# Projections of a hybrid decoder step in seven block products instead of eight, with K and V apart and the branch inputs through DRAM

## The reference

```python
h = rmsnorm(x, g_mix_pre)
q, k, v, cb, cc, cu, ga, gb = split(h @ w_in)      # 1024,128,128, 3 x 1024, 2 x 2048 columns
q, k = rope(q), rope(k)
a = window_attention(q, k, v, sinks)               # blocks of 128, 16 heads, 2 KV heads
b_out = cb * causal_dwconv(cc * cu)                # 3 taps
merged = sigmoid(ga + b0) * (a @ w_attn_branch) + sigmoid(gb + b1) * (b_out @ w_conv_branch)
x = x + rmsnorm(merged @ w_o, g_mix_post)
up, gt = split(rmsnorm(x) @ w_ffn_up)              # 2 x 5632 columns
x = x + rmsnorm((gelu(causal_dwconv(up) + b) * gt) @ w_ffn_down)
x = x + sigmoid(x @ w_ple_gate) * (p @ w_ple)
```

## Time and profile before

| what | us |
|---|---|
| median of 3 runs (2893.45 to 2894.02) | 2893.95 |
| the profiled execution | 2893.35 |
| its span, first to last instruction | 2891.7 |
| PE busy | 2784.8 (96%) |
| VectorE busy | 2024.4 (70%) |
| ScalarE busy | 1231.9 (43%) |
| GpSimd busy | 64.8 (2%) |
| mean granted clock of TensorE | 0.983 of 2.4 GHz |

### The profile page before, as it was taken

One profiled execution on the slowest core, in us unless ns is written; L12 is line 12 of the kernel. 1 busy time (PEld: TensorE's weight loads), 2 busy tenths in 40 slices (PEclk: granted clock), 3 DMA queues, 4 the chain that ended last, 5 costly groups with the idle time before them and its releaser, 6 DMA issues. The chain is left out here.

```text
span 2891.7 us, 57855 instructions
## 1 busy us (share of the span) xinstructions
PE 2784.8 (96%) x22023; PEld 2719.5 (94%) x22023; DVE 2024.4 (70%) x3439; ACT 1231.9 (43%) x2172; POOL 64.8 (2%) x67
## 2 busy tenths in 40 slices
PE   6999999999999999989999999999999999999789
PEld 6989999999999999978999999999998999989589
DVE  6355454333333358888888888888889788899988
ACT  4223323222222234545555555555555453445344
POOL 4110000000000000000000000000000000000000
PEclk8999999999999999999999999999999999999799
DMA  4222222233333333352333233332334243334343
GB/s 172 84 75 76 75 78 80 88 91 91 91 91 91 91 105 109 130 201 95 119 110 131 99 131 111 118 130 99 131 104 176 97 147 107 106 117 142 141 174 131
DMA packets 129393, 327.67 MB, mean 113 GB/s; under 512 B 15001, under 2 KB 35105, under 8 KB 126288
## 3 DMA queue, kind: packets, MB, share of 16 engines
q1 hardware_dynamic: 128992, 325.68, 33.3%
q0 software_dynamic: 288, 0.67, 0.1%
HBM read 297.13 MB, written 30.41 MB: 113 GB/s over the span
## 5 line engine op out<-in xcount | busy, mean ns | idle before, releaser
L907 PE MATMUL pair<-o_hi,v_hi 128*128 128x260 f32 x4270 | 1216.2, 285 | 36.0 <-DVE y_sb L1865 10.9
L907 PE MATMUL pair<-o_hi,v_lo 128*128 128x260 f32 x4270 | 1210.8, 284 | 0.0
L907 PE MATMUL pair<-lo,v_hi 128*128 128x260 f32 x3050 | 866.0, 284 | 0.0
L1132 ACT ACTIVATE v_hi<-s_raw 128x512 fp32r<-128x512 f32 (+1 forms) x944 | 585.8, 622 | 636.9 <-PE pair L907 612.2
L907 PEld LDWEIGHTS pair<-o_hi,v_hi 128*128 128x128 f32 x4270 | 808.7, 189 | 41.7 <-issue 23.2
L907 PEld LDWEIGHTS pair<-o_hi,v_lo 128*128 128x128 f32 x4270 | 809.8, 190 | 0.0
L1693 DVE TENSOR_TENSOR v_lo<-s_raw,v_hi 128x512 fp32r<-128x512 f32 (+1 forms) x944 | 638.2, 677 | 174.7 <-ACT v_hi L1132 139.5
L1402 DVE TENSOR_TENSOR w_lo<-w_raw,w_hi 128x512 fp32r<-128x512 f32 x328 | 238.9, 732 | 556.4 <-ACT w_hi L987 556.4
L907 PEld LDWEIGHTS pair<-lo,v_hi 128*128 128x128 f32 x3050 | 578.2, 190 | 0.2
L987 ACT ACTIVATE w_hi<-w_raw 128x512 fp32r<-128x512 f32 x328 | 206.7, 631 | 664.0 <-PE pair L660 646.7
L660 PE MATMUL pair<-h_hi,w_hi 128*128 128x260 f32 x2112 | 435.1, 287 | 22.0 <-DVE h_lo L1424 14.0
(11 more groups left out here) (219 smaller groups left out, 2722.7 us busy)
## 6 DMA issues: line engine op xcount, KB each, us to landing
s_raw<-in_sstream SPq DMA_DIRECT2D x308, 512.0 KB, 4.9
w_raw<-in_wstream SPq DMA_DIRECT2D x328, 256.0 KB, 2.6
s_raw<-in_sstream SPq DMA_DIRECT2D x32, 384.0 KB, 3.1
f_scr<-fo SPq DMA_DIRECT2D x88, 130.0 KB, 1.9
x_scr<-y_sb SPq DMA_DIRECT2D x8, 1040.0 KB, 4.2
raw<-f_scr SPq DMA_DIRECT2D x7, 1040.0 KB, 5.6
raw<-in_x SPq DMA_DIRECT2D x4, 1040.0 KB, 6.5
ple_scr<-ple_sb SPq DMA_DIRECT2D x4, 1040.0 KB, 4.8
```

Source lines behind the costliest of these rows:

```text
L907: mm = pe.matmul(out, wt[:, slot, kk * P:kk * P + P], r[:, k, :], start=j in (0, 1, 3) and k == 0 and n == 0, stop=k == nk - 1 and n == 2, ...
L1132: nc.scalar.activation(v_hi[:, n % 4, 0:width], src, ACT.Copy).then_inc(v_hi_rdy, 1)
```

## The change

The projections of Q, conv and gates become a set of 32 units of seven block products (set 0 with `U_O` = 32 units: 2 of gates, 4 of Q, 12 of conv, 14 of gates), written out in a line instead of in loops. K and V are made first, in native fp32, from rows of x as they arrive, x times the gain but not yet times the norm; the norm is then multiplied into the 16 rows in place (`h_row`), and the set begins. Everything that the attention and the branches need, and that stayed in SBUF before, goes through DRAM scratch: rotated Q (`q_scr`), b (`b_scr`), sigmoided gates (`g_scr`), attention output (`a_scr`). The attention is cut into 16 quarter blocks (two head pairs each) in place of 8 half blocks, one in each of the units of `ATT`. The two branches are 32 steps of 48 matmuls in the old three-matmul form, first all of the conv branch, then all of the attention branch. The squares of x are summed by VectorE and no longer by GpSimd, the rotation (cosine part) too; GpSimd issues the DMAs of the attention.

```diff
+U_Q, U_CONV, U_SIG = 2, 6, 18
+U_O, N_O = 32, KD // 2
+def kind(u):
+    return "g" if u < U_Q or u >= U_SIG else "q" if u < U_CONV else "CuB"[(u - U_CONV) % 3]
+ATT = {U_CONV + 7: 0, U_CONV + 10: 1, **{U_SIG + n: n + 2 for n in range(14)}}
...
 @block.tensor
+            for k in range(KD):
+                pe.wait_ge(x_rdy, k + 1)
+                for n, w in enumerate(quarter_of(k)[:2]):
...
+                        mm = pe.matmul(pair[2 + n][:, h, 0:HALF], w[:, quarter_of(k)[2]], x_half(k, h),
+                                       start=k == 0, stop=k == KD - 1, skip_group_check=True)
+                mm.then_inc(kv_used, 1)
...
+            def between(u):
+                if u - 1 in range(U_Q, U_CONV):
+                    r = 2 * (u - 1 - U_Q)
+                    return {0: lambda: rotate(r), 2: lambda: rotate(r + 1)}
+                if u == U_CONV + 1:
+                    return {0: v_turn, 1: lambda: rotate(KA)}
+                if u == U_CONV + 3:
+                    return {0: sample_scores, 5: sample_turn}
+                if u == U_CONV + 4:
+                    return {1: sample_values}
+                if u in ATT:
+                    n = ATT[u]
+                    return {-1: lambda: scores(n), 3: lambda: turn(n), 5: lambda: values(n)}
+                return {}
...
-            units(0)
+            first_unit(0)
+            for u in range(1, U_O):
+                unit(0, u, u % 2, between(u))
...
 @block.scalar
+            def exponentials(n):
+                act.wait_ge(m_ready, n + 1)
+                for h in range(4):
+                    nc.scalar.activation(s_sb[:, h, :], s_sb[:, h, :], ACT.Exp,
+                                         bias=small[:, 1, h:h + 1],
+                                         accum_out=small[:, 3, h:h + 1])
+                nc.scalar.activation(small[:, 4, 0:4], small[:, 2, 0:4], ACT.Exp)\
+                  .then_inc(e_ready, 1)
...
+            def h_evac(u, i):
+                d, k = d_h[u % 2], kind(u)
+                if u and kind(u - 1) == "g" and i in (0, 1):
+                    sigmoid_g(u - 1, i)
+                if i == (0 if is_first(u) else 1):
...
+                    copied(u, 0, d[:, 0, 0:HALF], r1_out)
+                if i == 3:
+                    copied(u, 1, d[:, 1, HALF:T], r5_out)
+                if i == 5:
+                    copied(u, 2, d[:, 0, HALF:T], r2_out)
+                if k == "B" and i == 2:
+                    conv_first((u - U_CONV) // 3)
...
+                if u in ATT and i == 4:
+                    exponentials(ATT[u])
+                if u in ATT and i == 9:
+                    turned(ATT[u])
+            by(0, h_evac)
...
 @block.vector
+            def h_row(k):
+                dve.wait_ge(kv_used, k + 1)
+                dve.tensor_tensor(x_tile(k), x_tile(k), two(rstd[:, :]), ALU.mult).then_inc(h_rdy, 1)
...
+            def h_evac(u, i):
+                if U_Q < u <= U_CONV:
+                    r = 2 * (u - 1 - U_Q)
+                    if i == 2:
+                        sine(r)
+                        cosine(r)
+                    if i == 3:
+                        turn_q(r)
+                    if i == 6:
+                        sine(r + 1)
+                        cosine(r + 1)
+                        turn_q(r + 1)
...
+                if k == "B":
+                    m = (u - U_CONV) // 3
+                    if i in (0, 1):
+                        conv_z(m, i)
+                    if i in (3, 6):
+                        conv_taps(m, i // 6)
+                if u and kind(u - 1) == "B" and i in (0, 1):
+                    conv_b((u - 1 - U_CONV) // 3, i)
...
+                if u in ATT:
+                    if i in (0, 1):
+                        masked(ATT[u], i)
+                    if i == 2:
+                        shifts(ATT[u])
+                    if i == 6:
+                        probabilities(ATT[u])
+                    if i == 12:
+                        attention_out(ATT[u])
+                sums(u, i, d[:, 0, 0:HALF], d[:, 0, HALF:T], d[:, 1, HALF:T])
...
 @block.sync
+            for u in range(U_O - 1):
+                h_store(u - 1)
+                load(r_of(u) + 2)
...
+            br_load(0)
...
+            br_load(1)
+            for m in range(NBR):
+                if m + 2 < NBR:
+                    sp.wait_ge(br_free, m + 1)
+                    g_load(m + 2)
+                if m % 4 == 3:
+                    load(R_BR + m // 4 + 2)
```

More of the change, by code:

```diff
@@ L109, in build @@
         r_raw4 = region(4 * HB)
[L110 to L131, removed]
+        r_op = region(10 * HB)
+        r_w = region((8 + 1) * KH * P * 4 + 2 * 4 * 4 * P * 4)
+        r_g = region(KD * XB)
+        r_c = top[0]
+        o = [r_w]
         def sub(name, shape, dt=f32):
@@ new lines, in _ @@
+            u = U_O - 1
+            h_store(u - 1)
+            for i in range(2):
+                sp.wait_ge(h_stored[i], 16 * stores_before(u - 1 + (i != (u - 1) % 2)))
+            sp.wait_ge(v_used, h_of(u, 1, 1) + 1)
+            br_load(0)
+            sp.wait_ge(b_rdy, KA)
+            g_load(0)
+            g_load(1)
+            load(r_of(u) + 2)
+            h_store(u)
+            sp.wait_ge(v_used, h_of(u, 6, 1) + 1)
+            for i in range(2):
+                sp.wait_ge(a_stored[i], 16 * 8)
+                sp.wait_ge(h_stored[i], 16 * stores_before(U_O + i))
@@ L565, in _ @@
             x_store(3)
-            load(u + 3)
+            load(r_of(U_UP) + 1)
             ple_store(2)
@@ L653, in _ @@
         def _(pe):
-            def products(acc, slot, kk, rhi, rlo, k, start, stop):
-                w = slice(kk * P, kk * P + P)
-                for wt, r, first, last in ((w_hi, rhi, True, False), (w_hi, rlo, False, False),
-                                           (w_lo, rhi, False, True)):
-                    for h in range(2):
-                        mm = pe.matmul(pair[acc][:, h, 0:HALF], wt[:, slot, w],
-                                       r[:, k, h * HALF:(h + 1) * HALF],
-                                       start=start and first, stop=stop and last)
-                return mm
@@ new lines, in _, with rotate @@
+            pe.wait_ge(sq_added, KD - 1)
+            pe.wait_ge(pool_set, 3)
+            for h in range(2):
+                mm = pe.matmul(pair[1][:, h, 0:HALF], ones[:, :],
+                               sqacc1[:, h * HALF:(h + 1) * HALF], start=True, stop=True)
+            mm.then_inc(sum_ready, 1)
+            def rotate(r):
+                u = U_Q + r // 2
+                if r < KA:
+                    for n in ((c11_out, c12_out), (c22_out, c21_out))[r % 2]:
+                        pe.wait_ge(n, u + 1)
+                    src = d_h[u % 2][:, r % 2, :]
+                else:
+                    src = k_in
+                pe.wait_ge(kv_out, 2)
+                if r:
@@ L1250, in _ @@
+            v_high(BR_S + 3)
+            sigmoid_g(U_O - 1, 0)
+            sigmoid_g(U_O - 1, 1)
+            warm(ACT.Sqrt, 2)
+            for m in range(NBR):
+                if m + 2 < NBR:
+                    v_high(BR_S + 2 * m + 4)
+                    v_high(BR_S + 2 * m + 5)
+                if 4 <= m < 4 + KA:
+                    br_high(1, m - 4)
+            by(1, wo_evac)
             y_square(U_UP - 1, 2)
@@ new lines, in masked @@
+            def masked(n, g):
+                if g == 0:
+                    dve.wait_ge(mask_ready[n >= 4], 16)
+                    if n:
+                        dve.wait_ge(pT_ready, 2 * n)
+                dve.wait_ge(sc_ready, 2 * n + g + 1)
+                for v in range(2):
+                    h = 2 * g + v
+                    ins = dve.tensor_tensor_reduce(
+                        s_sb[:, h, :], bank[g][:, v * 256:(v + 1) * 256], mask_blk[:, :],
+                        SCALE, -3.0e38, ALU.add, ALU.max, small[:, 0, h:h + 1])
@@ L1833, in unit @@
                 n = s_of(u, 0)
-                more = not last or u == U_UP - 1
+                ahead = 16 if u == U_O - 1 else 14 if last and u != U_UP - 1 else 18
                 for i in range(14):
-                    if i < 10 or more:
+                    if i + 4 < ahead:
                         v_low(n + i + 4)
@@ L2222 @@
                             range(16 * c + nk, 16 * c + 2 * nk)))
-    sparts.append(quads(tiles(wg, 0), tiles(wg, 1), lower, upper))
+    sparts.append(pairs_of(v["w_ple_gate"][0]))
     sstream = np.concatenate(sparts)
```

1401 lines of the change are left out of this document (660 added, 741 removed).

## The result

| what | before | after |
|---|---|---|
| median of 5 runs on the same chip | 2893.45 (2891.96 to 2894.02) | 2908.03 (2903.39 to 2908.42) |
| profiled execution, span | 2891.7 | 2905.9 |
| mean granted clock of TensorE | 0.983 | 0.970 |

The account below looks back on a forecast made before the run. TensorE (PE) was taken to set the pace nearly everywhere. w_o would start at 968.5 + 63 + 26 + 18 = 1075.5 us, 14 later than 1061.7, giving 2893.95 + 14 = 2908 us; eight-in-ten range 2840 to 2926.

Parts of the forecast that it names:

- Waits for the probabilities: Attention quarters: TensorE stands 13 times 4.2 us with a table load in the chain, 3 times 2.8 without: 63 us.
- Half clock: Attention units: after each of the 13 long waits matmuls run slow, 2 us each: 26 us, bounds 0 and 33.
- Convolution, rotations, samples: First stage: added VectorE steps make small waits, mainly for the sum before half 12: 18 us, bounds 0 and 30.
- the four in the B units: Four units with two convolution taps and small steps on VectorE: about 2.4 us late each, 9 us.
- Start and matmuls: First stage without new waits: first row at 44.4 us, third unit at 111.5, w_o at 968.5, 93 us less.
- 605 + 67 + 184 + 1: From the third unit to w_o: 30 units of 20.16 us, kept TensorE work, the branches, and 1 at w_o.
- the clock stays: Rival, chance 0.25: attention waits come but the clock does not fall, and small waits cost 5 us less: 2877 us.
- The test set for it: Sign for the clock rival: whether the granted clock is over 0.95 in 650 to 1000 us.
- the steps fit: Rival, chance 0.12: ScalarE and VectorE get ahead, TensorE stands under 1 us in an attention quarter: 2827 us.
- A late start: Rival, chance 0.07 shared with starved units: K and V at half clock throughout, ending 24 us later: 2932 us.
- starved units: Rival sharing chance 0.07 with a late start; the DMA estimate said that without cover a unit waits for its 5 us load.
- a load costs double: Rival, chance 0.06: ScalarE drains another 1.28 us for each of 13 table loads, 17 us: 2925 us.

Follow-up runs that it names:

- experiment 7: Changed kernel with probabilities at step 4 of VectorE's list, transposes after product 4, and gates by tanh instead of sigmoid: 2813.81 us.
- experiment 3: Changed kernel with the probabilities at step 4 instead of 6 of VectorE's list, before two weight slots' low parts: 2839.26 us.
- experiment 1: Changed kernel with the first set's gates taking Exp in place of Sigmoid (another function, only timed), so no table switches: 2871.31 us.
- experiment 5: Changed kernel with ScalarE starting the exponentials at step 3 of its list instead of step 4: 2906.98 us.
- experiment 6: Changed kernel with VectorE's taps, second rotations and sample copies moved behind the sum of the lower right block: 2897.9 us.
- experiment 8: Changed kernel with probabilities at step 4, transposes after product 4, tanh gates, and VectorE's other steps behind the lower right sum: 2805.6 us.
- experiment 4: Changed kernel with both moves: transposes after product 4 and probabilities at step 4 of VectorE's list: 2828.45 us.

## Why the prediction was right

The periods put the terms apart. In units with gates:

| run | wait for probabilities | period | over 23.55 | over the wait |
|---|---|---|---|---|
| 7 (no wait, no loads) | 0 | 23.55 | 0 | 0 |
| 3 | 1.55 | 25.40 | 1.85 | 0.3 |
| 1 | 2.45 | 27.44 | 3.89 | 1.4 |
| the change | 3.88 | 29.59 | 6.04 | 2.2 |

(a period is the distance between the first and the thirteenth quarter of these units, by 12).

*Waits for the probabilities.* Predicted 13 of 4.2 us with a table load in the chain and 3 of 2.8: 63. Measured 13 of 3.88 and 3 of 2.45: 57.7. The count was 0.3 us too high for each of them: from the start of the high part (662.43) TensorE stands after 4.3 us and not after 4.1, so the 0.2 taken off for the semaphore was most of it, and it starts again after 8.2 and not 8.3. The difference between the kinds is 1.43 us, against my 1.4. The chain was the right one: load, exponentials, two high parts, two low parts, probabilities. Experiment 1 takes out the first link, 3 the low parts, and 5 shows that moving only the exponentials inside the chain brings nothing.

*Half clock.* Predicted 2 us for each long wait, 26 in all, and none for the three shorter ones. By the last column it is 2.2 for each of the 13, 28 us, of which up to 0.3 is the restart that experiment 3 shows at full clock. The three of 2.45 us had it as well, some 1.4 each by experiment 1, 4 us. The term is 32 instead of 26, and the step that failed a little is the reading of the earlier trace rows: I let the first attention block, with 2.82 us and no fall, speak for the three. Such a wait was not always followed by it (11 of 16 times in experiment 1), so that these 4 us could have been less in another run. So both attention terms together are 90 us, and 89 were forecast.

*Convolution, rotations, samples.* Predicted 18 us. The listed waits in these units are 11.0 + 2.1 + 0.2 = 13.3 us, and 13 restarts of about 0.3 (an estimate, from experiment 3) make 17. One stretch of half clock, which I did not forecast, lies behind waits of 2.08 and 0.96 us at the samples' softmax (0.59 granted from 289 to 291 us, 0.56 from 291 to 293), about 1.5 more: 19. Their parts were less good: the four in the B units were 1.6 us, not 2.4, the rotations 0.6, not 0.9. Experiment 6 shows that they come from the steps ahead of the sum.

*Start and matmuls.* The first row of h was used at 45.3 us (44.4 predicted), half 12 of the second unit began at 105.0 (44.4 + 60.9 + 1.3 = 106.6 by the prediction's terms) and the third unit, 24 matmuls on, at 109.5 (111.5), the branches took 184.5 us from 890.9 to 1075.4 (184), and w_o began at 1075.4 (1075.5). From there it is 1830.5 us to the end, as before. In experiment 8, the third unit starts at 109.3 us and w_o at 972.7. Of these 863.4 us, 4.1 are listed waits and about 1.5 half clock behind the softmax, which leaves 858; the prediction's 605 + 67 + 184 + 1 is 857. A unit without attention takes 20.4 us there (three units with one quarter are 425.52 - 361.15 = 64.37 us, less 23.55, by two), with a wait of 0.24 us in every third; 20.2 was said. So matmuls and kept work were right, and the start was 2 us shorter than forecast.

*The rivals.* That the clock stays would have given 2877. The test set for it, over 0.95 from 650 to 1000 us, was a poor one: some 110 us of that stretch are branches at 1.00, and its mean is 0.95. In the attention units alone (640 to 900 us) it is 0.92, and it fell behind all thirteen long waits. That the steps fit would have given 2827; experiment 4 makes that case, with 0.66 us of waiting in a quarter: 2828. A late start is out, since K and V ran from 8.0 to 38.7 us, and so are starved units: no wait of TensorE from 100 to 1060 us was ended by a DMA. That a load costs double is out: the load at 663.08 begins 0.02 us after the high part's end, it lasts 1.28, and its removal shortens the wait by 1.43. The drain of 1.38 us that the Trainium skill (ScalarE: Activation LUTs, What ACT_TABLE_LOAD costs) adds to each switch is not seen here. The rule of the Trainium skill (the same page, Table sets), to batch by set, holds: the loads cost 37 us of the changed kernel by experiment 1, with the clock that follows. There are 27 of them from 500 to 900 us, 13 before exponentials and 14 before sigmoids; the prediction's "26 between 600 and 900" had the stretch wrong.

So the change does bring what its count of matmuls says, 93 us up to w_o, and 2 more at the start. The new order gives back 109: some 58 in waits for the probabilities, 32 in half clock and restarts behind them and 19 in the small waits. That w_o began within 0.1 us of the forecast is luck: the start was 2 us too long and the waits together 2 us too short. Most of what was given back was order and one function's table, not work: experiment 7, with both moves and tanh, keeps every matmul and gets some 93 us back.

## What to carry to other kernels

Work that is moved from a queue with free time into a densely pipelined unit is priced by the chain through all engines' lists, from the link that makes it possible to the one that wants it; here 2.3 us of a 3.9 us wait were unrelated steps that had slack of their own. Before splitting such a chain, look at where the consumer asks: one line that let TensorE ask a product later was worth 76 us. And count what follows a long stand of TensorE as part of its price: 3.88 us cost 6.0.

## What was not expected

Waits of 2.45 us were followed by the 1.2 GHz level in all three places of the change, in two of three in experiment 6 and in 11 of 16 in experiment 1, where two waits of one length, 26 us apart, went both ways. In experiment 5 one of two waits of 2.48 us was followed by it, and one of 3.03 us, which ended at 490.38, was not. Before, a stand of 2.82 us had not been either; there by stretches of 2 us (us, TensorE's busy time and records, granted clock, DMA share, GB/s):

```profile
212.00:214.00 2.00, 2.00 (x10) 1.00 0.29 111
214.00:216.00 2.00, 2.00 (x15) 1.00 0.00 0
```

None of the thirteen waits of 1.55 us in experiment 3 was, and every one of the 3.88 us of the change and of the 3.94 us of experiment 5. So from about 2.4 to 3 us the length of the wait alone doesn't decide it, and no run here settles what else does.

A wait of 0.66 us in the view was worth 1.16 us a unit (experiments 4 and 7), so the view understates short waits. And the steps of experiment 6 gave 10.1 us on the change and 8.2 on top of experiment 7. The traces show that this is not the steps: from half 12 of the second unit to the first exponentials of the gate units, they are worth 9.8 us in the one pair (413.05 and 403.26) and 9.6 in the other (398.05 and 388.50). The rest lies ahead of it, in a start that no edit touches and that varies: half 12 begins at 103.5 us in experiment 7 and at 104.8 in experiment 8, and between 103.4 and 105.1 in the change and experiments 1 to 8.
